# Gate and up weights four rows to a partition, with three of a pair's four units in one 4 MB transfer each from the sixth pair of experts on

## The chip, the cores and the metric

The kernel runs on one core of one Trainium2 chip. The metric is the device time of one execution in microseconds (us); a median over runs is given. The profile is of one execution. Engines are named as the profile names them: PE is TensorE (PEld its weight loads), DVE is VectorE, ACT is ScalarE, POOL is GpSimd, SP is the sync engine, which issues nearly all transfers. A pair, below, is a pair of experts.

## What is computed

One layer of an encoder block for 256 tokens of 1024 channels, all in float32: an attention and pooling part (the first 190 us), and then a mixture of experts, where the rest of the time goes. Each of the 32 experts has a gate/up matrix (1024 by 2048, 8 MB) and a down matrix (1024 by 1024, 4 MB). Each token goes to 4 experts.

```python
gu = xb @ w_gate_up[e] + b_gate_up[e]
gate = jnp.minimum(gu[:, :EXPERT_DIM], SWIGLU_LIMIT)
up = jnp.clip(gu[:, EXPERT_DIM:], -SWIGLU_LIMIT, SWIGLU_LIMIT)
act = gate * jax.nn.sigmoid(SWIGLU_ALPHA * gate) * (up + 1.0)
return act @ w_down[e] + b_down[e]
```

The outputs are scaled by the token's gate and summed into the residual `x`.

## The kernel before

**Weights and slots.** All weights of the experts are read once, in units of 2 MB, into ten slots of 16 KB in each of 128 partitions. A gate/up matrix is four units (`gu_slot`, eight slots for the two experts of a pair), a down matrix two (`dn_slot`, two slots). Gate/up unit `i` holds rows 256i to 256i+255 of the matrix; partition p of the slot has rows 2p and 2p+1 of these, which lie together in memory, so each partition's piece is one run of 16 KB (`gu_src`, L231). A down unit has four rows of 4 KB to a partition, also one run of 16 KB. Row r of the weights multiplies channel r of the activations, so which rows lie in a partition sets which channels the kernel has to gather into it: `gather_first`, `gather_rest` and `gather` (L1265 to L1319) turn `xn` with a matmul whose stationary operand is every second channel, and `g2_t`, the channel gains of the second norm, is loaded by POOL in the same order (L390).

**The order of the work on PE.** `pair` (L1431) runs one turn: `gate_up(1)` for the second expert of this pair (units 4 to 7), with the scatter of earlier results after k 1 and k 3, a turn of the gates after k 4 and the gather for the next pair after k 6; `down(0, 0)`, `turn`, `down(0, 1)` for the first expert; `gate_up(0)` for the first expert of the next pair (units 0 to 3) with two more scatters; and `down(1, 0)`, `turn`, `down(1, 1)`. Each unit is two values of k. `gate_up` waits for `gu_in[s]` before the first of the two (L1369) and raises `gu_used[s]` after the second. Turn 1 stands alone, a loop runs turns 2 to n-1 (`pe.Fori(2, n)`, L1468) and the last turn n has its own form, in which `x_in_sums` takes the gather's place and `add_to_sums` and `last_down` end the kernel. n is 16 here.

**The order of the transfers.** SP issues them in the order in which PE wants them, each when its slot is free. The first eight gate/up units and two down units are loaded while the attention part ends and frees their slots: units 0 to 7 in this order (L306 to L319), then the down units (L320). The next gate/up load waits for `first_used`, which PE raises after the first k of `gate_up` (L344). Up to pair `EARLY` = 5 the order is spelled out; then a loop (L362) issues for each pair

```python
gates_a(here, q)
downs_b(sp.snap(2 * (it % PAIRS)), q2)
gates_b(here, q)
downs_a(here, q3)
```

where `gates_a` and `gates_b` are four units each, `downs_a` and `downs_b` two. After the loop the last expert's down matrix goes into `gu_slot[0]` and `gu_slot[1]`, in three transfers (L370, L373).

Of the kernel before, what the change touches and what calls it, by code (L numbers as in the profile page):

```python
# [5 lines left out]
P = 128  # L6
SEQ = 256
D = 1024
NB = SEQ // P
KC = D // P  # L10
# [52 lines left out]
def block_kernel(nc, x_d, pos_d, w_in, w_a, w_b, w_out, mix_d, router_d, w_gu, w_dn, b_dn,  # L63
# [6 lines left out]
    with ctx:  # L70
        def sb(name, width, dt=f32, parts=P):
            return ctx.enter_context(nc.sbuf_tensor(name, [parts, width], dt))

        def sem(name):
            return ctx.enter_context(nc.semaphore(name))
# [7 lines left out]

        slot = [sb(f"slot{s}", UW) for s in range(SLOTS)]
        gu_slot = [slot[s] for s in (0, 1, 6, 7, 3, 9, 4, 8)]
        dn_slot = [slot[5], slot[2]]
# [88 lines left out]
        p1_copied, gate_done = sem("p1_copied"), sem("gate_done")  # L175
        gu_in = [sem(f"gu_in{s}") for s in range(GU_SLOTS)]
        gu_used = [sem(f"gu_used{s}") for s in range(GU_SLOTS)]
        dn_in = [sem(f"dn_in{j}") for j in range(DN_SLOTS)]
# [43 lines left out]
        def pre_unit_src(u):  # L222
# [6 lines left out]
            return w[r:r + 2 * P, :].rearrange("(k p) n -> p k n", p=P), 2 * D  # L229

        def gu_src(e, i):  # L231

            return w_gu[bass.ds(e * D + i * 2 * P, 2 * P), :].rearrange("(p k) n -> p (k n)", k=2)

# [25 lines left out]
        def _(sp):  # L260
# [52 lines left out]
            load_gu(4, 1)  # L313
            sp.wait_ge(job_ready, 2 * (BJ_WB + NB))
            load_gu(5, 1)
            units_used(18)
            load_gu(6, 1)
            sp.wait_ge(job_ready, 2 * (BJ_WA + NB))
            load_gu(7, 1)  # L319
            for j in range(DN_SLOTS):  # L320
# [8 lines left out]
            def gates_b(expert, used, first=0, end=4):  # L329
                for i in range(first, end):  # L330
                    sp.wait_ge(gu_used[4 + i], used)
                    load_gu(4 + i, expert + 1)

            def downs_a(expert, used):
# [27 lines left out]
            with sp.Fori(EARLY - 1, n - 1) as it:  # L362
                here, q, q2, q3 = sp.snap(2 * ((it + 1) % PAIRS)), sp.snap(it + 1), sp.snap(2 * it + 2), sp.snap(2 * it + 3)
                gates_a(here, q)
                downs_b(sp.snap(2 * (it % PAIRS)), q2)
                gates_b(here, q)
                downs_a(here, q3)
# [12 lines left out]
        @block.gpsimd  # L380
        def _(pool_e):
            pool_e.wait_ge(unit_in[0], 16)
            pool_e.dma_start(consts[:, P:K_W], consts_d[:, P:K_W]).then_inc(small_in, 16)
            pool_e.dma_start(rows[:, :], rows_d.to_broadcast([P, R_W])).then_inc(small_in, 16)
            pool_e.dma_start(posi[:, :], pos_d).then_inc(small_in, 16)
            pool_e.wait_ge(unit_in[2], 16)
            pool_e.dma_start(bands_t, bands_d).then_inc(late_in, 16)
            pool_e.dma_start(mixw, mix_d.rearrange("g c d -> c g d")).then_inc(late_in, 16)
            pool_e.dma_start(bgu_t[:, :], bgu_d).then_inc(bgu_in, 16)
            for k in range(2):  # L390
                for m in range(2):
                    pool_e.dma_start(g2_t[64 * m:64 * m + 64, k:KC:2],
                                     cols_d[k:P:2, P_G2 + m:P_G2 + KC:2], allow_slow_non_contiguous=True).then_inc(g2_in, 16)

            pool_e.wait_ge(t_ready, TJ_M + 4)
            for h in range(2):
                pool_e.dma_start(bd_sb[E * h:E * h + E, :], b_dn[:, 512 * h:512 * h + 512]).then_inc(bd_in, 16)

            pool_e.wait_ge(merged_ready, NB)
            pool_e.dma_start(rw, router_d.rearrange("(k p) e -> p k e", p=P)).then_inc(rw_in, 16)  # L400
# [149 lines left out]
        def _(dve):  # L550
# [412 lines left out]

            dve.wait_ge(g2_in, 64)
            take_xgT(1)
# [20 lines left out]
        def _(pe):  # L986
            MM = nc.tensor.matmul
            for j in range(DN_SLOTS):
                pe.sem_inc(dn_used[j], 1)
            for j in range(4):  # L990
                pe.sem_inc(done[f"Y{j}"], 2)
# [273 lines left out]
            def gather_first(h):  # L1265
                pe.wait_ge(sel_ready, 1)
                pe.wait_ge(xn_ready, 2 * NB)
                for k in range(4):
                    c0 = (4 * h + k) // 2 * 2 * P + k % 2
                    MM(XY[h][:, k * P:k * P + P], xn[:, 0, c0:c0 + 2 * P - 1:2], selb[:, 0:P], start=k == 0, stop=False)  # L1270

            def gather_rest():
                pe.wait_ge(sel_ready, 2)
                pe.wait_ge(xn_ready, 3 * NB)
                for h in range(2):
                    for k in range(4):
                        c0 = (4 * h + k) // 2 * 2 * P + k % 2
                        ins = MM(XY[h][:, k * P:k * P + P], xn[:, 1, c0:c0 + 2 * P - 1:2], selb[:, P:2 * P], start=False, stop=k == 3)
                    ins.then_inc(done[f"X{h}"], 1)
# [28 lines left out]
            def gather(count, freed):  # L1308

                pe.wait_ge(sel_ready, count)  # L1310
                for h in range(2):
                    pe.wait_ge(read[f"Y{2 + h}"], freed)
                for h in range(2):
                    for k in range(4):
                        c0 = (4 * h + k) // 2 * 2 * P + k % 2
                        for b in range(NB):
                            ins = MM(XY[h][:, k * P:k * P + P], xn[:, b, c0:c0 + 2 * P - 1:2], selb[:, b * P:b * P + P],  # L1317
                                     start=b == 0, stop=b == NB - 1)
                    ins.then_inc(done[f"X{h}"], 1)  # L1319
# [40 lines left out]

            def gate_up(e, landed, copied, taken, between, whole_first=False):
                for h in range(2):
                    pe.wait_ge(gu_copied[h], copied)
                for k in range(KC):
                    s = 4 * e + k // 2
                    if e == 0 and k % 4 == 0:
                        pe.wait_ge(read[f"X{k // 4}"], taken)
                    if k % 2 == 0:
                        pe.wait_ge(gu_in[s], landed)  # L1369
# [60 lines left out]

            def pair(count, turn_no, first, last):  # L1431
                q, q1 = count(turn_no + 0), count(turn_no + 1)
# [8 lines left out]
                else:  # L1441
                    between.append((6, lambda: gather(count(turn_no + 2), q3)))
                gate_up(1, in1, q2, None, between)
                down(0, 0, dn_a, q2, q2)
                turn(q3, q2)
                down(0, 1, dn_a, q2, q2)
                if not last:
                    gate_up(0, in2, q3, q1, [(1, lambda: scatter_a(0, q1, q3, q4, first)), (3, lambda: scatter_a(1, q1, q3, q4, first))])
                if last:
# [17 lines left out]
            n = pe.value_load(n_t[0:1, 0:1], min_val=PAIRS, max_val=4 * PAIRS)  # L1467
            with pe.Fori(2, n) as it:  # L1468
                pair(pe.snap, it, False, False)
            pair(pe.snap, n, False, True)  # L1470
            pe.wait_ge(last_copied, 1)
# [51 lines left out]
```

## Time and profile before

| what | value |
| --- | --- |
| median of 3 runs | 1099.01 us (1098.03 to 1099.58) |
| time of the profiled execution | 1100.01 us |
| span of the profiled execution | 1098.2 us |
| PE busy | 1051.5 us (96%) |
| weights and inputs read from memory | 429.03 MB |
| gate/up transfers of 2 MB, median issue to landing | 127, 29.4 us |

The span is the time from the first to the last instruction of the profiled execution; the 1.8 us between it and the execution's time lie around the instructions. A busy share is an average over stages with different limits. In the queries below, a stretch of time is given in us from the span's start.

### The profile page before, as it was taken

To read this page: it belongs to the slowest core of one execution; us is meant where nothing else is said; L and a number is where in the kernel's file an instruction comes from. 1 tells how busy PE (TensorE), PEld (TensorE's weight loads), DVE (VectorE), ACT (ScalarE), POOL (GpSimd) and SP (SyncE) were. 2 spreads that over 40 slices of the span, in tenths; PEclk is the share of its full clock that TensorE was granted. 3 is DMA by queue.
4 is the path that set the end of the run, shared out by engine and by line. 5 is a ranking of instruction groups with operands and counts; after the bars stand their busy time and mean duration, and the time that the engine had idled before them with its cause. 6 is when DMAs were issued, how large, how long until landed. Compare 5 with 4: busy or idle time off the path is not lost.

```text
span 1098.2 us, 12167 instructions
## 1 busy us (share of the span) xinstructions
PE 1051.5 (96%) x4822; PEld 425.5 (39%) x4822; DVE 356.0 (32%) x675; ACT 117.6 (11%) x211; POOL 8.2 (1%) x17
## 2 busy tenths in 40 slices
PE   9999999999999999999999999898989899999997
PEld 6445446333433434343433333242424242333322
DVE  4797224122222232322322322222222222122222
ACT  3115112100000000000000000000000000000001
POOL 2000000000000000000000000000000000000000
PEclk9999999999999999999999999999999999999999
DMA  9905784999999999999999999999999999999996
GB/s 326 376 28 192 290 363 176 407 422 416 427 429 429 429 428 429 428 429 427 428 429 429 428 428 429 428 428 428 429 429 428 428 430 428 428 428 428 429 428 251
DMA packets 40561, 430.33 MB, mean 392 GB/s; under 512 B 4048, under 2 KB 6224, under 8 KB 15712
## 3 DMA queue, kind: packets, MB, share of 16 engines
q1 hardware_dynamic: 39568, 428.11, 93.0%
q0 software_dynamic: 688, 1.91, 0.5%
q8 instruction: 12, 0.20, 0.1%
q10 hardware_dynamic: 288, 0.08, 0.0%
q14 instruction: 5, 0.04, 0.0%
HBM read 429.03 MB, written 1.05 MB: 392 GB/s over the span
## 4 chain that ended last, share of the span: by engine, by line
PE 63%; DMA 34%; SPq 2%; issue 1%; DVE 0%; ACT 0%; DVEq 0%
DMA slot<-w_gate_up_dram 33%; PE bank L1373 21%; PE bank L1400 14%; PE bank L1317 5%; PE bank L1185 4%; PE bank L1038 4%; PE bank L1062 4%; PE bank L1389 2%; PE bank L1334 2%; PE bank L1295 1%; SPq L290 1%; PE bank L1005 1%; PE bank L1427 1%; DMA x<-x_dram 1%; PE bank L1358 0%
## 5 line engine op out<-in xcount | busy, mean ns | idle before, releaser
L1373 PE MATMUL bank<-slot,scr 128*64 128x512 f32 x2048 | 469.9, 598 | 24.9 <-DMA slot<-w_gate_up_dram 24.7
L1373 PEld LDWEIGHTS bank<-slot,scr 128*64 128x64 f32 x2048 | 136.5, 136 | 322.8 <-issue 258.1
L1400 PE MATMUL bank<-slot,scr 128*64 128x512 f32 x992 | 225.4, 596 | 11.3 <-DMA slot<-w_down_dram 10.5
L947 DVE TENSOR_TENSOR x<-bank,x 128x512 f32<-128x512 f32 x120 | 77.3, 686 | 233.5 <-PE bank L1334 233.5
L1400 PEld LDWEIGHTS bank<-slot,scr 128*64 128x64 f32 x992 | 67.7, 137 | 142.3 <-issue 118.5
L922 DVE COPY scr<-bank 128x512 f32<-128x512 f32 x32 | 22.1, 692 | 288.2 <-PE bank L1373 288.2
L928 DVE TENSOR_TENSOR scr<-bank,bgu 128x512 f32<-128x512 f32 x64 | 41.2, 686 | 106.0 <-PE bank L1389 106.0
L1334 PE MATMUL bank<-scr 64*128 64x512 f32 x240 | 67.7, 641 | 0.0
L1317 PEld LDWEIGHTS bank<-scr,xn 128*128 128x128 f32 x480 | 57.7, 196 | 12.2 <-issue 12.2
L514 ACT ACTIVATE scr<-bank 128x512 f32<-128x512 f32 x32 | 19.1, 598 | 399.0 <-PE bank L1373 399.0
L1317 PE MATMUL bank<-scr,xn 128*128 128x128 f32 x480 | 60.5, 285 | 0.0
L1038 PE MATMUL bank<-slot,scr 128*128 128x290 f32 (+1 forms) x128 | 43.8, 501 | 0.4 <-DVE scr L573 0.3
L1389 PEld LDWEIGHTS bank<-consts,scr 128*128 128x128 f32 x256 | 33.4, 210 | 26.9 <-issue 26.9
L1389 PE MATMUL bank<-consts,scr 128*128 128x128 f32 x256 | 39.4, 297 | 0.9 <-ACT scr L514 0.9
L518 ACT ACTIVATE scr<-scr 128x512 f32<-128x512 f32 x32 | 20.2, 631 | 183.4 <-DVE scr L932 183.4
L1334 PEld LDWEIGHTS bank<-scr 64*128 64x128 f32 x240 | 18.1, 184 | 48.6 <-issue 48.6
L1038 PEld LDWEIGHTS bank<-slot,scr 128*128 128x128 f32 x128 | 24.0, 190 | 19.2 <-issue 15.3
L526 ACT ACTIVATE scr<-bank 128x512 f32<-128x512 f32 x16 | 9.6, 597 | 189.7 <-PE bank L1358 189.7
L1062 PE MATMUL bank<-slot 128*128 128x512 f32 x64 | 28.7, 596 | 0.0
L1185 PE MATMUL bank<-slot 128*128 128x512 f32 x56 | 26.4, 600 | 0.0
L522 ACT ACTIVATE scr<-bank 128x512 f32<-128x512 f32 x31 | 18.5, 598 | 45.3 <-PE bank L1400 45.3
L936 DVE SCALAR_TENSOR_TENSOR scr<-scr 128x512 f32<-128x512 f32 x32 | 22.2, 693 | 3.3
(202 smaller groups left out, 489.9 us busy)
## 6 DMA issues: line engine op xcount, KB each, us to landing
slot<-w_gate_up_dram SPq DMA_DIRECT2D x127, 2048.0 KB, 29.4
slot<-w_down_dram SPq DMA_DIRECT2D x63, 2048.0 KB, 22.8
slot<-w_in_dram SPq DMA_DIRECT2D x12, 1024.0 KB, 15.5
slot<-w_out_dram SPq DMA_DIRECT2D x4, 1024.0 KB, 7.3
slot<-w_in_dram SPq DMA_DIRECT2D x4, 580.0 KB, 7.8
slot<-w_branch_pool_dram SPq DMA_DIRECT2D x2, 1024.0 KB, 7.3
slot<-w_branch_attn_dram SPq DMA_DIRECT2D x2, 1024.0 KB, 6.2
slot<-w_gate_up_dram SPq DMA_DIRECT2D x2, 1024.0 KB, 5.8
```

Of the source, the lines that this page charges most:

```text
L922: V.tensor_copy(gu_sb[:, 512:1024], GB[1][:, :]).then_inc(gu_copied[1], 1)
L928: V.tensor_tensor(gu1[:, 4 * h:4 * h + 4, :, :], v4(TU[h][:, :], 4, 2), bias.unsqueeze(3).to_broadcast([P, 4, 2, T]), ALU.add).then_inc(re ...
L936: V.scalar_tensor_tensor(out=up1, in0=up1, scalar=1.0, in1=gu1[:, :, 0, :], op0=ALU.add, op1=ALU.mult).then_inc(prod_ready, 1)
L947: V.tensor_tensor(x[:, b, 512 * h:512 * h + 512], XY[h][:, :], x[:, b, 512 * h:512 * h + 512], ALU.add).then_inc(read[f"Y{j}"], 1)
L1038: ins = MM(bank[PAIR[j][b]][:, 0:n], hT[:, kc, b * P:b * P + P], w[:, k, :], start=kc == 0, stop=kc == KC - 1)
L1062: ins = MM(bank[PAIR[j][h]][:, :], lhs[:, k, b * P:b * P + P], w[:, k % 2, 512 * h:512 * h + 512], start=k == 0, stop=k == nk - 1)
L1185: ins = MM(acc[:, :], lhs[:, k, :], rhs[:, k, :], start=k == 0, stop=k == 3)
L1317: ins = MM(XY[h][:, k * P:k * P + P], xn[:, b, c0:c0 + 2 * P - 1:2], selb[:, b * P:b * P + P], start=b == 0, stop=b == NB - 1)
L1334: MM(XY[h][:, :], selgT[T * h:T * h + T, SEQ * e + b * P:SEQ * e + b * P + P], dsb[T * h:T * h + T, 512 * e:512 * e + 512], start=not with ...
L1373: ins = MM(GB[h][T * g:T * g + T, :], xgT[:, k, T * e:T * e + T], gu_slot[s][:, c0:c0 + 512], start=k == 0, stop=k == KC - 1)
L1389: ins = nc.tensor.transpose(TU[h][:, k * P:k * P + P], gu_sb[:, c0:c0 + 4 * P - 3:4], ident)
L1400: ins = MM(DB[T * h:T * h + T, :], actT[e][:, c, :], v3(dn_slot[j][:, :], 4)[:, k, 512 * h:512 * h + 512], start=c == 0, stop=c == KC - 1)
```

## The change

The memory of the ten slots becomes one tensor, so that two neighbouring slots can be written by one transfer. Four rows of a gate/up matrix, 32 KB, now lie over one partition of two neighbouring slots (a tile); a unit is half of such a tile, 16 KB out of every 32 KB. The slots of gate/up units 5, 6 and 7 change places, and with them the order of the first loads. From the loads for the sixth pair on, SP issues tiles 0, 1 and 2 (units 0 and 1, 2 and 3, 4 and 5) as one transfer of 4 MB each, with a semaphore of its own, and units 6 and 7 as before. PE waits for the whole tile before its first k. PE's one loop over turns becomes a loop over turns 2 to 4, turn 5 by itself, a loop over turns 6 to 15, and the last turn. The gathers take every fourth channel, and the gains are loaded by 16 small transfers in place of 4.

```diff
-        slot = [sb(f"slot{s}", UW) for s in range(SLOTS)]
-        gu_slot = [slot[s] for s in (0, 1, 6, 7, 3, 9, 4, 8)]
+        ring = sb("ring", SLOTS * UW)
+        slot = [ring[:, UW * s:UW * s + UW] for s in range(SLOTS)]
+        gu_slot = [slot[s] for s in (0, 1, 6, 7, 3, 4, 8, 9)]
+        gu_tile = [ring[:, UW * s:UW * s + 2 * UW] for s in (0, 6, 3, 8)]
...
+        big_in = [sem(f"big_in{t}") for t in range(3)]
...
+        def tile_src(e, t):
+
+            return w_gu[bass.ds(e * D + t * 4 * P, 4 * P), :].rearrange("(p k) n -> p (k n)", k=4)
+
         def gu_src(e, i):

-            return w_gu[bass.ds(e * D + i * 2 * P, 2 * P), :].rearrange("(p k) n -> p (k n)", k=2)
+            whole = tile_src(e, i // 2)
+            return whole[:, UW * (i % 2):UW * (i % 2) + UW]
...
             load_gu(4, 1)
             sp.wait_ge(job_ready, 2 * (BJ_WB + NB))
+            load_gu(7, 1)
+            units_used(18)
             load_gu(5, 1)
-            units_used(18)
+            sp.wait_ge(job_ready, 2 * (BJ_WA + NB))
             load_gu(6, 1)
-            sp.wait_ge(job_ready, 2 * (BJ_WA + NB))
-            load_gu(7, 1)
...
+            def tiles(expert, t, used):
+                for i in range(2):
+                    sp.wait_ge(gu_used[2 * t + i], used)
+                sp.dma_start(gu_tile[t], tile_src(expert + t // 2, t % 2)).then_inc(big_in[t], 16)
...
-                gates_a(here, q)
+                tiles(here, 0, q)
+                tiles(here, 1, q)
                 downs_b(sp.snap(2 * (it % PAIRS)), q2)
-                gates_b(here, q)
+                tiles(here, 2, q)
+                gates_b(here, q, 2, 4)
                 downs_a(here, q3)
...
-            for k in range(2):
-                for m in range(2):
-                    pool_e.dma_start(g2_t[64 * m:64 * m + 64, k:KC:2],
-                                     cols_d[k:P:2, P_G2 + m:P_G2 + KC:2], allow_slow_non_contiguous=True).then_inc(g2_in, 16)
+            for k in range(4):
+                for m in range(4):
+                    pool_e.dma_start(g2_t[32 * m:32 * m + 32, k:KC:4],
+                                     cols_d[k:P:4, P_G2 + m:P_G2 + KC:4], allow_slow_non_contiguous=True).then_inc(g2_in, 16)
...
+            for t in range(3):
+                pe.sem_inc(big_in[t], 16 * EARLY)
...
-                        c0 = (4 * h + k) // 2 * 2 * P + k % 2
+                        c0 = 4 * P * h + k
                         for b in range(NB):
-                            ins = MM(XY[h][:, k * P:k * P + P], xn[:, b, c0:c0 + 2 * P - 1:2], selb[:, b * P:b * P + P],
+                            ins = MM(XY[h][:, k * P:k * P + P], xn[:, b, c0:c0 + 4 * P - 3:4], selb[:, b * P:b * P + P],
                                      start=b == 0, stop=b == NB - 1)
...
-                    if k % 2 == 0:
+                    if whole and k % 4 == 0 and s < 6:
+                        pe.wait_ge(big_in[2 * e + k // 4], landed)
+                    elif k % 2 == 0 and not (whole and s < 6):
                         pe.wait_ge(gu_in[s], landed)
...
-            with pe.Fori(2, n) as it:
+            with pe.Fori(2, EARLY) as it:
                 pair(pe.snap, it, False, False)
-            pair(pe.snap, n, False, True)
+            pair(int, EARLY, False, False, whole_a=True)
+            with pe.Fori(EARLY + 1, n) as it:
+                pair(pe.snap, it, False, False, whole_b=True, whole_a=True)
+            pair(pe.snap, n, False, True, whole_b=True)
```

## Rows read from the trace of the kernel before

**Rows 1.** The page: PE's totals, and the memory rate in 40 slices.

```profile
PE 1051.5 (96%) x4822; PEld 425.5 (39%) x4822; DVE 356.0 (32%) x675; ACT 117.6 (11%) x211; POOL 8.2 (1%) x17
...
GB/s 326 376 28 192 290 363 176 407 422 416 427 429 429 429 428 429 428 429 427 428 429 429 428 428 429 428 428 428 429 429 428 428 430 428 428 428 428 429 428 251
```

**Rows 2.** Stretches of 58.7 us: busy time (and instructions) by engine, clock, DMA, GB/s.

```profile
434.80:493.50 58.70, 58.70 (x300) 24.54 (x300) 15.87 (x28) 4.25 (x7) 0.00 (x0) 1.00 1.01 428
...
669.60:728.30 58.70, 54.59 (x262) 20.26 (x260) 15.86 (x28) 4.21 (x8) 0.00 (x0) 1.00 1.01 428
```

**Rows 3.** Chain of waits, 419 to 473 us: start, duration, what.

```profile
419.08 3.43 PE bank L1373 x16
...
428.21 1.87 PE bank L1373 x8
...
430.67 3.58 PE bank L1373 x16
...
448.27 3.43 PE bank L1373 x16
...
457.40 7.02 PE bank L1373 x32
...
472.60 3.43 PE bank L1373 x16
```

**Rows 4.** Timeline of PE, 1002 to 1090 us: start, duration, [idle before, who ended it].

```profile
1002.79 1.94 PE L1373 MATMUL bank<-slot,scr 128*64 128x512 f32 x8 [0.19 <-DMA slot<-w_gate_up_dram]
...
1007.68 1.94 PE L1373 MATMUL bank<-slot,scr 128*64 128x512 f32 x8 [0.50 <-DMA slot<-w_gate_up_dram]
...
1056.62 3.65 PE L1373 MATMUL bank<-slot,scr 128*64 128x512 f32 x16 [0.18 <-DMA slot<-w_gate_up_dram]
...
1061.51 1.94 PE L1373 MATMUL bank<-slot,scr 128*64 128x512 f32 x8 [0.18 <-DMA slot<-w_gate_up_dram]
...
1066.67 1.94 PE L1373 MATMUL bank<-slot,scr 128*64 128x512 f32 x8 [0.76 <-DMA slot<-w_gate_up_dram]
...
1082.42 7.09 PE L1427 MATMUL bank<-slot,scr 128*64 128x512 f32 x32
```

**Rows 5.** What SP waited for, 350 to 1045 us: us in total, times, longest.

```profile
SPq L293 <- PE bank L1400: 599.0, 48, 24.0
```

**Rows 6.** Timeline of SP, 1000 to 1098 us.

```profile
1024.37 1.91 SPq L290 DMA_DIRECT2D slot<-w_gate_up_dram  x4
1045.78 5.22 SPq L293 DMA_DIRECT2D slot<-w_down_dram  x2
```

**Rows 7.** DMA view, stretches 600 to 1050 us and 26 to 51 us.

```profile
DMA packets 13243, 192.86 MB, mean 429 GB/s; under 512 B 1472, under 2 KB 1472, under 8 KB 1472
...
DMA packets 4792, 9.70 MB, mean 388 GB/s; under 512 B 148, under 2 KB 148, under 8 KB 4791
```

**Rows 8.** The page, DMA queues: the instruction queue's packets, MB, share.

```profile
q8 instruction: 12, 0.20, 0.1%
```

**Rows 9.** DMA view, 1055 to 1066 us, the instruction queue.

```profile
q8 instruction: 1, 0.02, 0.6%
```

**Rows 10.** Source view, L1317 and L1389: duration of one in ns (min/median/max), first and last start.

```profile
L1317 PEld LDWEIGHTS bank<-scr,xn x480: 193/196/197, 218.0 to 1013.2; 128*128 128x128 f32 x160
...
L1389 PEld LDWEIGHTS bank<-consts,scr x256: 195/212/219, 203.9 to 1076.6; 128*128 128x128 f32 x128
```

**Rows 11.** Timeline, 184 to 191 us, and a stretch of 2 us in it.

```profile
184.81 2.15 PE L1278 MATMUL bank<-scr,xn 128*128 128x128 f32 x16 [0.45 <-DVE scr L862]
...
189.07 0.33 SPq L345 DMA_DIRECT2D slot<-w_gate_up_dram  x1
...
188.00:190.00 2.00, 2.00 (x12) 0.84 (x10) 1.73 (x7) 0.00 (x0) 0.00 (x0) 1.00 0.00 0
```

**Rows 12.** POOL: its timeline at 14 us, and its longest wait.

```profile
13.77 2.46 POOL L392 DMA_DIRECT2D g<-cols_dram  x4
...
POOL scr L397 <- PE bank L1005: 138.9, 1, 138.9
```

More of the change, by code:

```diff
@@ L962, in pair @@
                     make_sel(after2)
-            dve.wait_ge(g2_in, 64)
+            dve.wait_ge(g2_in, 256)
             take_xgT(1)
@@ L1268, in gather_first @@
                 for k in range(4):
-                    c0 = (4 * h + k) // 2 * 2 * P + k % 2
-                    MM(XY[h][:, k * P:k * P + P], xn[:, 0, c0:c0 + 2 * P - 1:2], selb[:, 0:P], start=k == 0, stop=False)
+                    c0 = 4 * P * h + k
+                    MM(XY[h][:, k * P:k * P + P], xn[:, 0, c0:c0 + 4 * P - 3:4], selb[:, 0:P], start=k == 0, stop=False)
             def gather_rest():
@@ L1276, in gather_rest @@
                     for k in range(4):
-                        c0 = (4 * h + k) // 2 * 2 * P + k % 2
-                        ins = MM(XY[h][:, k * P:k * P + P], xn[:, 1, c0:c0 + 2 * P - 1:2], selb[:, P:2 * P], start=False, stop=k == 3)
+                        c0 = 4 * P * h + k
+                        ins = MM(XY[h][:, k * P:k * P + P], xn[:, 1, c0:c0 + 4 * P - 3:4], selb[:, P:2 * P], start=False, stop=k == 3)
                     ins.then_inc(done[f"X{h}"], 1)
@@ L1314, in gather @@
                     for k in range(4):
-                        c0 = (4 * h + k) // 2 * 2 * P + k % 2
+                        c0 = 4 * P * h + k
                         for b in range(NB):
-                            ins = MM(XY[h][:, k * P:k * P + P], xn[:, b, c0:c0 + 2 * P - 1:2], selb[:, b * P:b * P + P],
+                            ins = MM(XY[h][:, k * P:k * P + P], xn[:, b, c0:c0 + 4 * P - 3:4], selb[:, b * P:b * P + P],
                                      start=b == 0, stop=b == NB - 1)
@@ L1359, in gates_by_slot, with gate_up @@
                 ins.then_inc(done["S"], 1)
-            def gate_up(e, landed, copied, taken, between, whole_first=False):
+            def gate_up(e, landed, copied, taken, between, whole_first=False, whole=False):
                 for h in range(2):
@@ L1429, in last_down, with pair @@
                 ins.then_inc(dn_used[1], 1)
-            def pair(count, turn_no, first, last):
+            def pair(count, turn_no, first, last, whole_b=False, whole_a=False):
                 q, q1 = count(turn_no + 0), count(turn_no + 1)
@@ L1442, in pair @@
                     between.append((6, lambda: gather(count(turn_no + 2), q3)))
-                gate_up(1, in1, q2, None, between)
+                gate_up(1, in1, q2, None, between, whole=whole_b)
                 down(0, 0, dn_a, q2, q2)
@@ L1447, in pair @@
                 if not last:
-                    gate_up(0, in2, q3, q1, [(1, lambda: scatter_a(0, q1, q3, q4, first)), (3, lambda: scatter_a(1, q1, q3, q4, first))])
+                    gate_up(0, in2, q3, q1, [(1, lambda: scatter_a(0, q1, q3, q4, first)), (3, lambda: scatter_a(1, q1, q3, q4, first))], whole=whole_a)
                 if last:
```

## The prediction

> **What bounds the kernel now.** I read the page first. PE is busy 96% of the span and the memory rate is flat at 428 to 429 GB/s from the twelfth slice on [rows 1], so two resources look full, and the share can't say which one sets the end. Stretches of 58.7 us tell them apart [rows 2]: up to about 550 us PE has no idle time and more instructions fit a stretch than one turn of the loop needs (300 against 262), so PE runs ahead at its own pace; later PE is busy 54.6 of 58.7 us, and the stream still runs at the same 428 GB/s. The chain of waits gives PE's own pace: one turn from 419.08 to 472.60 us, 53.5 us [rows 3]. The timeline gives the other: unit 7 of two successive turns starts at 1007.68 and 1066.67 us, 59.0 us apart [rows 4]. So from some 550 us to the last weights the stream of transfers is the bound, and PE waits a little for each unit. What sets the end is: when the stream starts, how long it runs, and how much PE work is left when the last pieces have landed.
>
> Two facts about the stream. First, its step. Between 600 and 1050 us, 13243 - 1472 = 11771 packets of 16 KB went through 16 engines in 450 us: 450 x 16 / 11771 = 611.7 ns each, eight to an engine and unit, so 4.89 us per unit [rows 7]. Nothing is left over for a cost per transfer. Second, its depth: SP hardly waits for anything but down slots (599 us in 48 waits) [rows 5], since the gate/up slots of a turn have always been used by the time the down slots ahead of them in SP's order are free. A gate/up unit lands 29.4 us, six steps, after its issue (the table above). The change therefore issues nothing later: a tile's two waits are met when SP reaches them.
>
> **Longer rows in the stream.** No row shows a 32 KB packet. The cost of one is bounded by the packets that are there: between 26 and 51 us, 4644 packets with a mean of 2088 bytes took 25 x 16 / 4644 = 86.1 ns each, beside 611.7 ns for 16384 bytes [rows 7]. A straight line through both has 9.3 ns per packet and the rest by bytes. A tile in 32 KB packets needs 8 per engine where two units need 16, so it saves 8 x 9.3 = 75 ns. The loop issues 3 tiles in each of 11 turns: 33 x 0.075 = 2.5 us. The bounds: nothing, if the hardware cuts a row at 16 KB, and 3.3 us, if the line's constant is a third too low. I take 2.3 us. The ordinary units now read 16 KB out of each 32 KB; the nearest strided reads are those of 26 to 51 us, rows of `w_in` at a pitch of 14.6 KB (3652 floats), and even if all of the line's constant of 9.3 ns were due to their stride it would be 1.5% of a 16 KB packet; since the contiguous units fit the same line, I take nothing for it here.
> [...]
>
> **The hold of a whole tile.** PE now waits for 4 MB before the first of four k. The second half of a tile lands when the second unit landed, so the start of its four k is put off by one step, 4.89 us less what PE waited anyway. In the bound stretch that costs nothing as long as PE catches up in each turn. Count from the landing of tile 2 (units 4, 5). From there to the end of `down(0, 1)` PE needs 448.27 - 419.08 = 29.2 us [rows 3], and the next tile 0 lands six steps later, 29.4 us. Tile 0's work is 9.1 us (two units and their scatters), against 9.8 to tile 1. From tile 1 it needs 15.2 us (472.60 - 457.40), and tile 2 lands four steps later, 19.6. So PE is back at a standstill each turn, with 4.4 us to spare. The down slots come free later than before (in the last turn before from 1045.78 us on [rows 6]), but at least 10 us ahead of the time when the stream gets to them, because two tiles are still queued in front. The stream doesn't run dry.
>
> At the end nothing comes after to catch up in. Before, PE starts unit 5 at 1056.62 us and unit 7 at 1066.67, each as it lands, and from there on works without waiting for a transfer [rows 4]. Now it starts unit 4 when unit 5 is there, at 1056.62, and needs 9.13 us for units 4 and 5 with two scatters (428.21 - 419.08), 2.46 for k 4 with the turn of the gates, and 1.79 for k 5, half of the 3.58 [rows 3]. That makes 1070.00 us for the start of unit 7, against 1066.67: **3.3 us later**, and all that follows (`last_down` at 1082.42 and the sums) is PE's own work, so it moves by the same. Bounds: 2.5 (if a restart after a wait runs tighter than the back-to-back rows) to 4.9, a full step.
>
> **The start of the stream.** Between the first loads and the reload there is a hole, zero GB/s from 188 to 190 us: SP waits for `first_used` and issues at 189.07 us [rows 11]. That follows from `gather_rest` (16 matmuls, 2.15 us from 184.81), which is on the path. Its stationary reads go from every second to every fourth channel. L1317 loads every second element and takes 196 ns, `turn` at L1389 loads every fourth and takes 212 [rows 10]. So 16 loads x 16 ns is 0.26 us at most, 0 if the matmuls hide it; I take 0.2. In the loop 32 loads x 16 ns = 0.5 us a turn more, which the 4.4 us to spare take up; without that cover it would be 5 us over ten turns.
> The trace agrees in direction with the Trainium skill (SBUF — State Buffer, Specifications): a 16-byte line wants at least two hits for full bandwidth, and a step of four floats hits each line once. If that meant half speed, 196 ns a load would become 392 and the start would move 3.1 us; the row of `turn` has 212.
>
> **Code.** PE's program has 9644 records of matmuls and loads [rows 1], 522 to a turn [rows 2], so about 1290 before the turns and, with three written turn bodies, 2860 in all; 12 instruction fetches brought them in [rows 8]. The two new bodies (turn 5 and the second loop) are 1044 more, so four or five fetches, most inside the saturated stream. One such fetch, between 1055 and 1066 us, took 0.6% of 11 us x 16 engines, 1.06 us of engine time [rows 9], and there the step from unit 6 to unit 7 (1061.51 to 1066.67) is 5.16 us, 0.27 longer than 4.89 [rows 4]. A transfer has landed when its slowest engine is done, so a fetch costs nothing (on an engine with time in hand) up to 1.06 us. Five cost 0 to 5 us; by the one seen, 1.3. I take 1.0.
>
> **At nothing.** The order of the first loads (4, 7, 5, 6): same bytes, slots and waits; all of them are issued before `gather_rest` (184.81 us, [rows 11]), and `gate_up(1)` comes a whole `gate_up` after it. If unit 6 were late, PE would wait a step, 4.9 us, once, at a time when the stream, not PE, sets the end. The 12 further gain loads: 2.46 / 4 = 0.6 us each on POOL [rows 12], 7.4 us, ahead of a wait of 138.9 us; uncovered, 7.4 us. 22 fewer issues on SP, which idles 599 us.
>
> **The sum.** -2.3 + 3.3 + 0.2 + 1.0 = +2.2 us. On the profiled execution's span of 1098.2 that is 1100.4, on its 1100.01 us 1102.2; it stood 1.0 above the median of 1099.01, which becomes **1101.2 us**. About 0.2% (2.2 us) is what a measurement of this kernel can tell from no change, so the forecast sits on that edge.
>
> **The rivals.**
> *Rows are cut at 16 KB* (the change doesn't do what it says): nothing is saved, +4.5 us, 1103.5. For it: every packet of the stream is 16 KB or less. Against it: 16 KB is also the longest row that was asked for.
> *Transfers have a fixed cost in the stream* (faster): 33 fewer ones save it. The nearest row is SP's step between issues, 1.91 / 4 = 0.48 us [rows 6], so 33 x 0.48 = 15.8 us: 1101.2 - 15.8 = 1085.4. It gives a faster kernel from 4.4 / 33 = 0.13 us per transfer on. Against it: eight packets make the whole step [rows 7]. The Trainium skill (DMA: Bandwidth & Descriptors, Anatomy of one DMA) has such a cost, about 2 us per transfer, mostly completion; with six transfers queued the trace shows it overlapped.
> *The pitch slows the half-tile units*: 128 - 66 in tiles - 8 first loads = 54 of them lie in the saturated stream. At the 388 GB/s of 26 to 51 us [rows 7] each takes 5.4 us, 0.5 more: +27, 1128. Nothing in the trace shows such a pitch.
> *The hold isn't caught up*: if a turn ends later than the stream allows, each of ten turns loses up to a step of 4.9: +49, 1150. It decides only if PE needs 4.4 us more per turn than rows 3 say.
>
> **How the numbers follow.** The forecast has 0.68 (own range 1099.5 to 1103.0, about evenly on both sides of the edge), cut rows 0.14, a fixed cost 0.08, pitch 0.05, the hold 0.05. The range 1098.8 to 1104.6 takes in the first two with the bounds of fetches and restart. Slower: 0.30 + 0.14 + 0.05 + 0.05 = 0.54; same: 0.36; faster: 0.08 + 0.02.
>
> **What the profile after would show.** Packets over 16 KB and fewer of them, and a rate near 432 GB/s in stretches with tiles; PE idle only before tiles, about 4 us before tile 2; unit 7 of the last turn with no wait before it; `last_down` 13.4 + 15.8 = 29.1 us after tile 2's first k; 16 or 17 fetches; L1317's successor near 212 ns. It would be wrong if the rate didn't rise, if the stretch of full PE work before 550 us grew, or if PE waited for unit 6 or 7 in the last turn.

## The result, and the profile after

The changed kernel takes 1119.41 us (median of 4 runs, 1119.22 to 1119.83) against 1099.02 us before: a ratio of 1.0184, 95% interval 1.0172 to 1.0197, 20.4 us slower. The forecast was 1101.2 us, within 1098.8 to 1104.6. The way was right, the size was not, by far. The reason is one term, the stationary loads of the gathers, which the forecast had at 0.2 us for the start and at nothing for the turns.

The page of the changed kernel: its span, PE's totals, the memory rate in 40 slices, the queues (packets, MB, share), and three groups of instructions (busy, mean ns of one | idle before).

```profile
span 1117.8 us, 12107 instructions
...
PE 1101.7 (99%) x4822; PEld 486.6 (44%) x4822; DVE 355.6 (32%) x675; ACT 117.7 (11%) x211; POOL 14.2 (1%) x29
...
GB/s 332 362 34 197 295 328 171 410 384 399 389 421 385 421 387 426 375 430 430 430 430 429 437 424 438 423 435 426 432 429 432 430 432 430 430 430 429 426 430 225
...
q1 hardware_dynamic: 34816, 428.11, 91.5%
...
q8 instruction: 16, 0.26, 0.1%
...
L1392 PE MATMUL bank<-ring,scr 128*64 128x512 f32 x2048 | 466.2, 597 | 6.4 <-DMA ring<-w_gate_up_dram 6.4
...
L1334 PEld LDWEIGHTS bank<-scr,xn 128*128 128x128 f32 x480 | 113.1, 329 | 12.2 <-issue 12.2
...
L1408 PEld LDWEIGHTS bank<-consts,scr 128*128 128x128 f32 x256 | 33.3, 210 | 26.9 <-issue 26.9
```

Against [rows 1], PE has the same 4822 matmuls and 50.2 us more of them, PEld 61.1 us more. L1334 is the gather, L1317 of before. Its stationary load takes 329 ns; it took 196 [rows 10], and the forecast had 212. The matmuls with gate/up weights (L1392) take as long as ever, and PE waits only 6.4 us before them; `turn` (L1408) has the 210 ns it had. And the memory rate, flat from the twelfth slice before, dips to 375 to 389 GB/s in every other slice from the ninth to the seventeenth.

The chain of waits has one gather of the loop whole (start, duration), between units 6 and 7:

```profile
449.14 3.58 PE bank L1392 x16
452.73 7.66 PE bank L1334 x32
460.39 1.87 PE bank L1392 x8
```

7.66 us a turn where it was 3.97 (32 matmuls of L1317 at 434.25 us in the chain of before); PE's own turn (two starts of the same step, 609.20 and 666.42 us) is 57.2 us in place of 53.5 [rows 3].

Stretches of 20 us, columns as in [rows 2], first of the changed kernel and then of the kernel before:

```profile
230.00:250.00 20.00, 20.00 (x92) 6.79 (x90) 6.61 (x11) 1.83 (x3) 0.00 (x0) 1.00 0.90 371
250.00:270.00 20.00, 20.00 (x96) 6.89 (x92) 6.68 (x13) 1.83 (x3) 0.00 (x0) 1.00 0.99 396
...
350.00:370.00 20.00, 20.00 (x94) 6.83 (x92) 6.01 (x10) 1.23 (x2) 0.00 (x0) 1.00 0.91 366
...
450.00:470.00 20.00, 20.00 (x94) 12.11 (x92) 5.04 (x9) 1.23 (x2) 0.00 (x0) 1.00 0.87 357
```

```profile
230.00:250.00 20.00, 20.00 (x90) 6.19 (x88) 4.14 (x7) 1.11 (x2) 0.00 (x0) 1.00 1.00 426
250.00:270.00 20.00, 20.00 (x94) 6.82 (x90) 7.97 (x15) 1.83 (x3) 0.00 (x0) 1.00 1.01 415
...
350.00:370.00 20.00, 20.00 (x96) 6.94 (x94) 6.68 (x13) 1.82 (x3) 0.00 (x0) 1.00 1.01 429
...
450.00:470.00 20.00, 20.00 (x94) 6.83 (x92) 4.52 (x7) 0.60 (x1) 0.00 (x0) 1.00 1.01 429
```

The last two columns (the share of time in which the transfer engines were busy, and GB/s) are the point: PE has no idle time in either kernel, but now the transfer engines have. SP can refill a slot only when PE has used it. That a whole turn of 57.2 us is still shorter than the stream's 58.7 doesn't help, for two reasons that SP's timeline shows. Down weights have two slots, and SP issues in order, so what counts is the time from one pair of down loads to the next. And up to pair `EARLY` the spelled-out order puts four gate/up units between two pairs of down loads, then three: six and five units with the down units, 29.4 and 24.5 us of stream at 4.89 us each, 53.8 us a turn. SP's timeline before the change:

```profile
253.80 5.08 SPq L293 DMA_DIRECT2D slot<-w_down_dram  x2
258.92 13.41 SPq L290 DMA_DIRECT2D slot<-w_gate_up_dram  x4
282.99 5.08 SPq L293 DMA_DIRECT2D slot<-w_down_dram  x2
288.11 8.03 SPq L290 DMA_DIRECT2D slot<-w_gate_up_dram  x3
307.32 5.07 SPq L293 DMA_DIRECT2D slot<-w_down_dram  x2
```

and after it, with a stretch of 2 us at the end of the long half:

```profile
261.20 5.07 SPq L301 DMA_DIRECT2D ring<-w_down_dram  x2
266.31 13.41 SPq L298 DMA_DIRECT2D ring<-w_gate_up_dram  x4
294.08 5.08 SPq L301 DMA_DIRECT2D ring<-w_down_dram  x2
299.20 8.03 SPq L298 DMA_DIRECT2D ring<-w_gate_up_dram  x3
318.42 5.07 SPq L301 DMA_DIRECT2D ring<-w_down_dram  x2
...
294.00:296.00 2.00, 2.00 (x14) 1.35 (x14) 1.02 (x2) 0.00 (x0) 0.00 (x0) 1.00 0.63 131
```

Before, PE hands the down slots back after 29.2 and 24.3 us, which just feeds the stream. The gather lies in the longer half. Now that half takes 32.9 us, and the stream, with 29.4 us of work in hand, runs dry for some 3.5 us before each of the down loads at 294.08, 351.30, 408.51 and 465.96 us. By the same sum the first hole, before 234.76 us, is 2.9 us. That estimate makes 17 us in all. From the loop on there are six units to each half, 58.7 us of stream for PE's 57.2: PE's shorter half, 24.3 us, now leaves 5 us of transfers queued for the longer one, and the holes end. Over the 13 such stretches from 230 to 490 us the rates add up to 5201 GB/s in place of 5552, which at 428 is (5552 - 5201) x 20 / 428 = 16.4 us of stream lost. Later the stream is the bound again and goes at its own rate, so nothing of that comes back. The first wait of PE for a weight transfer in the pairs is at 781.91 us in the changed kernel (572.10 before), and from there on there is one in each of the six turns left. The timeline of PE in the last two turns shows it:

```profile
1015.92 3.65 PE L1392 MATMUL bank<-ring,scr 128*64 128x512 f32 x16 [1.06 <-DMA ring<-w_gate_up_dram]
...
1074.43 3.65 PE L1392 MATMUL bank<-ring,scr 128*64 128x512 f32 x16 [1.07 <-DMA ring<-w_gate_up_dram]
...
1103.63 7.09 PE L1446 MATMUL bank<-ring,scr 128*64 128x512 f32 x32
```

PE waits for tile 2 each time and its turns are 58.5 us apart, the stream's pace. So the sum, in the profile's own times: the reload starts 3.7 us later (SP's issue at 192.78 us against 189.07 [rows 11]), the holes cost 16.4, the longer rows give about 2.3 back, and the last turn's hold adds up to 3.3: 21.1 us for the start of `last_down`, which moved by 1103.63 - 1082.42 = 21.2 [rows 4]. The first three terms can be read by themselves: unit 5 is there 1074.43 - 1056.62 = 17.8 us later. The two spans are only 19.6 us apart, because in the profiled execution before the change the output took longer: 6.1 us from the first output transfer's issue (1092.08 us) to the end, where the changed kernel (1113.30 us) and all the other profiles have 4.4 to 4.5.

### The profile page after: what moved, and what is told of

Read it like the earlier page. It is cut to its first block, busy times and chain, and to the rows that moved or that the text cites. A ratio compares the mean times of both kernels' runs of the same rounds, so it can differ in the third digit from the quotient of the medians.

```text
span 1117.8 us, 12107 instructions
## 1 busy us (share of the span) xinstructions
PE 1101.7 (99%) x4822; PEld 486.6 (44%) x4822; DVE 355.6 (32%) x675; ACT 117.7 (11%) x211; POOL 14.2 (1%) x29
## 4 chain that ended last, share of the span: by engine, by line
PE 85%; DMA 14%; SPq 0%; issue 0%; ACT 0%; DVE 0%; DVEq 0%
PE bank L1392 33%; PE bank L1419 16%; DMA ring<-w_gate_up_dram 13%; PE bank L1334 10%; PE bank L1351 5%; PE bank L1202 4%; PE bank L1055 4%; PE bank L1079 4%; PE bank L1408 3%; PE bank L1312 1%; PE bank L1022 1%; PE bank L1375 1%; PE bank L1446 1%; DMA ring<-w_in_dram 1%; PE bank L1295 0%; PE bank L1434 0%
## 5 line engine op out<-in xcount | busy, mean ns | idle before, releaser
L1392 PE MATMUL bank<-ring,scr 128*64 128x512 f32 x2048 | 466.2, 597 | 6.4 <-DMA ring<-w_gate_up_dram 6.4
L1392 PEld LDWEIGHTS bank<-ring,scr 128*64 128x64 f32 x2048 | 137.9, 137 | 297.5 <-issue 283.2
L1419 PE MATMUL bank<-ring,scr 128*64 128x512 f32 x992 | 224.9, 595 | 0.0
L1419 PEld LDWEIGHTS bank<-ring,scr 128*64 128x64 f32 x992 | 68.4, 137 | 127.7 <-issue 124.0
L1334 PEld LDWEIGHTS bank<-scr,xn 128*128 128x128 f32 x480 | 113.1, 329 | 12.2 <-issue 12.2
L1334 PE MATMUL bank<-scr,xn 128*128 128x128 f32 x480 | 116.0, 400 | 0.0
L1408 PEld LDWEIGHTS bank<-consts,scr 128*128 128x128 f32 x256 | 33.3, 210 | 26.9 <-issue 26.9
L1055 PE MATMUL bank<-ring,scr 128*128 128x290 f32 (+1 forms) x128 | 43.8, 501 | 0.8 <-DMA ring<-w_in_dram 0.8
L1408 PE MATMUL bank<-consts,scr 128*128 128x128 f32 x256 | 39.3, 297 | 0.9 <-ACT scr L529 0.9
L1055 PEld LDWEIGHTS bank<-ring,scr 128*128 128x128 f32 x128 | 24.0, 190 | 19.6 <-issue 15.3
L1079 PE MATMUL bank<-ring 128*128 128x512 f32 x64 | 28.7, 596 | 0.0
L1202 PE MATMUL bank<-ring 128*128 128x512 f32 x56 | 26.4, 600 | 0.0
```

The costliest lines, as they stand in the source:

```text
L1055: ins = MM(bank[PAIR[j][b]][:, 0:n], hT[:, kc, b * P:b * P + P], w[:, k, :], start=kc == 0, stop=kc == KC - 1)
L1079: ins = MM(bank[PAIR[j][h]][:, :], lhs[:, k, b * P:b * P + P], w[:, k % 2, 512 * h:512 * h + 512], start=k == 0, stop=k == nk - 1)
L1202: ins = MM(acc[:, :], lhs[:, k, :], rhs[:, k, :], start=k == 0, stop=k == 3)
L1334: ins = MM(XY[h][:, k * P:k * P + P], xn[:, b, c0:c0 + 4 * P - 3:4], selb[:, b * P:b * P + P], start=b == 0, stop=b == NB - 1)
L1392: ins = MM(GB[h][T * g:T * g + T, :], xgT[:, k, T * e:T * e + T], gu_slot[s][:, c0:c0 + 512], start=k == 0, stop=k == KC - 1)
L1408: ins = nc.tensor.transpose(TU[h][:, k * P:k * P + P], gu_sb[:, c0:c0 + 4 * P - 3:4], ident)
```

## The experiments

Theory G says that all beyond the forecast is the gathers' stationary loads. Rival H puts it to the tiles, their hold or the pitch. The first four runs tell them apart.

**e1: the changed kernel, gathers at every second channel**

```diff
-                        c0 = 4 * P * h + k
-... xn[:, b, c0:c0 + 4 * P - 3:4] ...
+                        c0 = (4 * h + k) // 2 * 2 * P + k % 2
+... xn[:, b, c0:c0 + 2 * P - 1:2] ...
```

> The changed kernel whose gathers read every second channel, as before the change; the channels are then the wrong ones for the four-row weights, and nothing else differs. Theory G (the gathers' stationary loads): the gather falls back from 7.7 to 4.0 us a turn and the stream starts 3 us earlier, so the time is what was forecast without the gather's term: 1099 + 2 = 1101 us, 1099.5 to 1103. Rival H (the hold of whole tiles, or the 32 KB pitch of the half-tile units): these are untouched, so 1112 to 1119 us, and the stream still has its holes between 230 and 480 us.

1102.96 us, ratio 1.0039 (1.0024 to 1.0054). G's value, at the top of its range: 16.5 of the 20.4 us are gone with this one line, which stands in three places, and its memory rate has no such dips (426, 409, 428, 429 from the ninth slice on).

**e2: the kernel before, gathers at every fourth channel**

The same edit the other way round, in the kernel before.

> The kernel before, whose gathers read every fourth channel (the wrong ones for its two-row weights); nothing else differs. Theory G: PE's turn grows from 53.5 to 57.2 us, the stream starts 3 us later and gets holes while PE is the bound: 1114 to 1120 us. Rival H: 1099 to 1104 us, since a turn of 57.2 us is still under the stream's 58.7.

1118.42 us, ratio 1.0174 (1.0159 to 1.0190). The stride alone, with neither tiles nor four-row weights nor new turn bodies, makes 19 of the 20 us, holes in the stream included: its slices of the memory rate go 378, 404, 387, 421, 386, 419 like those above. "A turn of 57.2 us is still under the stream's 58.7" and so harmless, as H had it, is refuted: the sum over a turn is right, but the half of it with the gather is longer than the stream's six units.

**e3: the changed kernel with the activations written in the gather's order**

```diff
-  nc.scalar.activation(xn[:, b, :], x[:, b, :], ACT.Copy, scale=...)
+  nc.scalar.activation(xn[:, b, :].rearrange("q (h k p) -> q h k p", h=2, k=4),
+                       x[:, b, :].rearrange("q (h p k) -> q h k p", h=2, k=4), ACT.Copy, scale=...)
...
-  xn[:, b, 4 * P * h + k:4 * P * h + k + 4 * P - 3:4]
+  xn[:, b, (4 * h + k) * P:(4 * h + k) * P + P]
```

> The changed kernel in full, but ACT writes the normed activations in the order of the gather (channel 512h + 4p + k at place 512h + 128k + p), so each gather's stationary operand is 128 neighbouring floats. Theory G: a load takes 190 ns as in the other matmuls, the gather 3.9 us a turn, and the time is 1099.5 to 1103 us, or 0.3 us under the run that reads every second channel; ACT's two copies from the strided source may cost up to 1 us at the start. Rival H: 1112 to 1119 us.

1102.20 us, ratio 1.0032 (1.0020 to 1.0044). It is the change with the cost of its gather taken away. G's value again. The ratio puts it 3.5 us above the kernel before (2.2 to 4.8 by its interval), where the forecast's other terms had made 2.0 (2.2 less the gather's 0.2).

**e4: the load against its step**

In the kernel before, the eight groups of the loop's gather read 128 channels at steps of 1 to 8 floats (`xn[:, b, 0:127 * s + 1:s]`), each on its own line. Only the loads are read from it; its one execution took 1110.68 us.

> The kernel before, whose gather in the loop takes 128 channels at a step of 1, 2, 3, 4, 5, 6, 7 and 8 floats in its eight groups (the wrong channels), each on a line of its own, to measure a stationary load against its step. If what counts is how many 16-byte lines the 128 floats touch, a load takes 190 ns at 1, 196 at 2, 330 at 4, some 250 at 3, and 330 from 4 to 8. If it is the span in bytes, it grows on from 4 to 8: 600 ns and more at 8.

The source view of each line, PEld (ns: min/median/max); L1315 is step 1, L1330 step 8:

```profile
L1315 PEld LDWEIGHTS bank<-scr,xn x60: 186/190/192, 218.4 to 1021.5; 128*128 128x128 f32 x60
...
L1317 PEld LDWEIGHTS bank<-scr,xn x60: 195/197/200, 218.9 to 1022.0; 128*128 128x128 f32 x60
...
L1319 PEld LDWEIGHTS bank<-scr,xn x60: 251/261/263, 219.3 to 1022.6; 128*128 128x128 f32 x60
...
L1321 PEld LDWEIGHTS bank<-scr,xn x60: 317/330/330, 220.0 to 1023.5; 128*128 128x128 f32 x60
...
L1324 PEld LDWEIGHTS bank<-scr,xn x60: 314/315/319, 220.9 to 1024.4; 128*128 128x128 f32 x60
...
L1326 PEld LDWEIGHTS bank<-scr,xn x60: 316/317/319, 221.8 to 1025.2; 128*128 128x128 f32 x60
...
L1328 PEld LDWEIGHTS bank<-scr,xn x60: 325/327/328, 222.7 to 1026.2; 128*128 128x128 f32 x60
...
L1330 PEld LDWEIGHTS bank<-scr,xn x60: 334/334/335, 223.6 to 1027.1; 128*128 128x128 f32 x60
```

190, 197, 261, 330, and then 315 to 334: it isn't the span that counts. The time rises as long as fewer floats share 16 bytes and stops where each has its own, as expected of the number of 16-byte lines touched; the small steps between 315 and 334 that count doesn't explain. That is the direction of the rule of the Trainium skill (SBUF — State Buffer, Specifications) that the forecast cited: with two hits to a line (step 2) the load is nearly at full speed, with one (step 4) it takes 330/190 = 1.74 times as long.

What is left of e3's excess was then taken apart. Theory T: the hold in the last turn, and a clock that falls in it. Rival R: the new turn bodies, or the pitch.

**e5: e3 with 2 MB units and no holds**

`tiles(here, t, q)` is replaced by `gates_a(here, q)` and `gates_b(here, q)`, and PE waits for `gu_in[s]` in all turns.

> The changed kernel with ordered activations (the run e3 before), but every unit in a transfer of its own, 2 MB, waited for by itself; four-row weights, slots and PE's two loops stay. Theory T: what e3 still loses is the last turn's hold (3.3 us, and 1.7 us for 16 matmuls at half the clock after PE's idle 3.3 us), less 2.4 us that the 32 KB packets give. So 1102.2 - 5.0 + 2.4 = 1099.6 us, 1099 to 1100.3. Rival R (the new turn bodies and their fetches, or the 32 KB pitch, cost the 3 us): 1102 us or more.

1099.01 us, ratio 0.9997 (0.9988 to 1.0006): T. The four-row layout, the 32 KB pitch, the new bodies and the order of the first loads cost nothing that can be told, which leaves room for about 1 us.

**e5h: e5, with the holds put back**

```diff
+                    if whole and k % 4 == 0 and s < 6:
+                        pe.wait_ge(gu_in[s], landed)
+                        pe.wait_ge(gu_in[s + 1], landed)
+                    elif k % 2 == 0 and not (whole and s < 6):
+                        pe.wait_ge(gu_in[s], landed)
```

> The same with 2 MB units, but PE waits before the first k of units 0, 2 and 4 for that unit and its neighbour, from turn 5 or 6 on, as it would for a whole tile: the hold by itself, without the longer rows. Theory T: 5.0 us over the run with separate waits, 1104.6 us; the first matmuls of the last turn run at half the clock after an idle of 3 to 4 us. Rival: if the hold costs only its delay, 3.3 us, 1102.9; if PE catches up, no difference.

1104.42 us, ratio 1.0043 (1.0029 to 1.0056), 5.4 us over e5 by the medians. The hold costs more than the delay of 3.3 us. Timeline of PE in this run's last turn:

```profile
1057.59 5.35 PE L1391 MATMUL bank<-ring,scr 128*64 128x512 f32 x16 [4.32 <-DMA ring<-w_gate_up_dram]
...
1063.93 3.65 PE L1391 MATMUL bank<-ring,scr 128*64 128x512 f32 x16
```

After 4.32 us of idle time the first 16 matmuls take 5.35 us, the next 16, the same work, 3.65. The granted clock is the cause; in e3, the same place (stretches of 5 us; the column before the last two is the clock):

```profile
1050.00:1055.00 5.00, 2.42 (x12) 0.57 (x8) 3.38 (x8) 1.23 (x2) 0.00 (x0) 1.00 0.90 380
1055.00:1060.00 5.00, 4.31 (x12) 1.30 (x14) 0.00 (x0) 0.00 (x0) 0.00 (x0) 0.66 1.00 426
1060.00:1065.00 5.00, 5.00 (x24) 1.51 (x22) 1.29 (x2) 0.00 (x0) 0.00 (x0) 1.00 0.99 423
```

0.66 over five microseconds is a stay at the lower of the two levels, 1.2 GHz, and then the return to 2.4. In the kernel before, PE's longest wait for a unit in these turns is 1.25 us, and the page's clock row is full throughout.

**e9: e3 with tiles 0 and 1 only**

Units 4 to 7 are one by one again (`gates_b(here, q)`, and the hold only where `s < 4`).

> The run e3 with tiles 0 and 1 in 4 MB transfers as before and units 4 to 7 one by one, so that no hold lies in the last turn; 22 tiles in place of 33. Theory T: 1102.2 - 5.0 + 0.8 (11 tiles less at 0.073 us) = 1098.0 us, faster than before the change by about 1 us, and no long idle time ahead of unit 4. Rival R: 1101.5 to 1103.

1097.90 us, ratio 0.9989 (0.9980 to 0.9998). It is the fastest of all, 1.2 us below the kernel before; the interval just excludes no difference. But a hold still sets its end: PE idles 3.54 us ahead of tile 0 at 1026.27 us, takes 6.57 us for the next 16 matmuls, and from there on never waits for a transfer again, with unit 4 of the last turn at 1053.57 us. The expectation had no hold left in the last turn; its number came out all the same, and not by the path that it named.

**e7: the kernel before with ordered activations**

> The kernel before with the normed activations written in the order of its own gather (two rows to a partition): nothing of the change. A load takes 190 ns in place of 196, so the gather is 0.1 us shorter a turn and the start of the stream comes 0.1 us earlier at most; ACT's strided copies may take that back. 1098.8 to 1099.5 us, no difference that can be told.

1098.71 us, ratio 0.9995 (0.9986 to 1.0004). No difference that can be told, as expected (the median is 0.1 us under the range): e9's gain isn't the order of the activations by itself.

**e8: the kernel before, every fourth channel in the loop only**

> The kernel before, with only the loop's gathers reading every fourth channel (the wrong ones); the two gathers ahead of the mixture of experts read every second one. It splits the 19.2 us of the run in which all do. If the extra time is PE's work alone (15 gathers of 3.7 us on top of a PE that was idle for about 36 us, and 3.5 us of later start), this has all but the start: 1118.4 - 3.5 = 1114.9 us, 1114 to 1116. If the holes in the stream set the time by themselves and the start counts for nothing, 1118.

1115.96 us, ratio 1.0154 (1.0138 to 1.0169). The loop's gathers alone make 17 us, and they make it by the holes: the stream starts at 189.04 us as before the change, and the dips are there (386, 378, 381, 378, 382 GB/s in every other slice from the ninth on). The two gathers ahead of the loop add some 2 us, the rest of e2's 19, though the intervals of the two ratios overlap. Its value is just inside the range of the first view, 1 us above its centre.

**e5c: e5 with PE's one loop of before**

> The changed kernel with ordered activations, 2 MB transfers throughout and PE's one loop of before: what is left of the change is the four-row layout, the slots, the order of the first loads and the 16 small loads of the gains. It differs from the run with 2 MB units only in PE's two further turn bodies and their four instruction fetches. By the forecast's term (1.0 us for the fetches) 1098.0 us; if the fetches cost nothing, 1099.0, and the layout costs nothing either; if the 32 KB pitch cost anything, above 1099.5.

1098.83 us, ratio 0.9997 (0.9988 to 1.0006), the same as e5. Four fetches and two bodies cost nothing that can be told, and neither does the layout. The two intervals are about 1 us wide to each side, so the forecast's 1.0 us for the fetches isn't excluded.

**e11: e3 with tile 1 only**

> The run with tiles 0 and 1, but only tile 1 (units 2 and 3) in one transfer of 4 MB, 11 tiles in place of 22. The longer rows give 0.8 us less, 1097.9 + 0.8; but in that run tile 0's hold and the half clock after it made PE start the last turn's unit 4 at 1053.6 us, 2.9 after it landed, and unit 6 and 7 without a wait, so up to 1.7 us of it should go. 1097.0 to 1098.7 us. If it comes out above 1099, holding tile 1 costs the same as tile 0.

1099.61 us, ratio 1.0000 (0.9991 to 1.0009): a miss, above the expected 1097.0 to 1098.7. The kernel before took 1099.41 us beside this run and 1099.05 beside e9, so 0.4 of the 1.7 us between the medians of e9 and e11 lie in the kernel before as well. The trace shows what the expectation had wrong. PE at the last tile 1:

```profile
1037.87 8.54 PE L1391 MATMUL bank<-ring,scr 128*64 128x512 f32 x32 [3.55 <-DMA ring<-w_gate_up_dram]
```

32 matmuls of 7.09 us take 8.54, and PE then never waits for a transfer again, as in e9. But it comes to unit 4 of the last turn at 1054.42 us, 0.85 later than in e9 and not earlier, and the two profiled executions are 0.9 us apart. The hold of tile 1 ends 11.6 us later than that of tile 0, and leaves PE that much less time to catch up before the last turn. This is read from one execution of each, and the intervals of e9 and e11 overlap.

## Why the prediction was wrong, step by step

- **The step that failed: "16 loads x 16 ns" and "32 loads x 16 ns = 0.5 us", in the paragraph on the start of the stream.** The difference of 16 ns was taken between L1317, loads of ordinary matmuls, and L1389, loads of transposes. These are two kinds of load, and each has its own base. Both bases stood in the same trace, here in the source views of L1038 and L1358 of the kernel before, which read neighbouring floats:

```profile
L1038 PEld LDWEIGHTS bank<-slot,scr x128: 186/190/192, 7.2 to 51.0; 128*128 128x128 f32 x128
```

```profile
L1358 PEld LDWEIGHTS bank<-consts,scr x32: 138/140/142, 213.8 to 1063.5; 128*128 128x128 f32 x32
```

  So a step of two cost a matmul's load 196 - 190 = 6 ns, and a step of four cost a transpose's load 212 - 140 = 72 ns, half as much again. Compared like with like, the nearest row of the trace gave 72 ns and a factor of 1.5 for what had been called 16. The changed kernel shows more, 134 ns and 1.7. The forecast then used its 16 ns to set the rule of the Trainium skill (SBUF — State Buffer, Specifications) aside. Its own figure for that rule, 196 ns more a load, was too high, but nearer than 16: it had the start 3.1 us later, and 3.7 was measured. In the loop it would have been 32 x 196 = 6.3 us a turn, more than the 4.4 to spare, which the forecast didn't work out.
- **The second failure: the cover of 4.4 us a turn.** It was counted in the stretch where the stream is the bound, and there it held (PE waits 1.07 us a turn in the changed kernel, from 781.91 us on). Before that PE is the bound, and the stream lives on the slots that PE hands back. "The stream doesn't run dry" was checked for the later turns alone, by waits of SP from 350 us on [rows 5]; 16.4 us were lost between 230 and 490 us. The forecast had the two numbers that say so: PE needs 29.2 us from tile 2 to the end of `down(0, 1)`, the half of the turn with the gather, and the stream takes 29.4 for its six steps. That is 0.2 us to spare and not 4.4; the added work was 3.7. The sign that the forecast named for being wrong, a longer stretch of full PE work, is there: from 572.10 to 781.91 us. "5 us over ten turns", named for the case without cover, was too small by far.
- **The start**: 0.2 us was forecast; the reload is issued 3.7 us later. The 32 loads of the two gathers there take 330 ns in place of 196, 4.3 us in all of which waits hid some, and part of `gather_rest` ran at the lower clock: a granted 0.89, 0.50 and 0.75 in the stretches of 2 us from 186 to 192 us. How much of the 3.7 is the clock's stays open.
- **Longer rows: right.** 32 KB packets came. From 600 to 1050 us, 193.53 MB went through in place of 192.86 [rows 7], 0.35% more, which over the some 620 us from the first tile to the last is 2.2 us; 2.3 was forecast. The mean rate is 430 GB/s, where a rate near 432 had been named. "Rows are cut at 16 KB" is refuted. The DMA view of the changed kernel:

```profile
DMA packets 9954, 193.53 MB, mean 430 GB/s; under 512 B 1104, under 2 KB 1104, under 8 KB 1104
```

- **The hold at the end: right, and more.** From tile 2's first k to `last_down` 29.1 us were forecast; it took 1103.63 - 1074.43 = 29.2 in the changed kernel. The 3.3 us was the delay alone; with a fast gather PE idles 3.28 us first in e3 (4.32 in e5h), and the clock adds 1.7 (5.35 - 3.65). The forecast's "back at a standstill each turn" missed that a standstill has a price. In the changed kernel itself that price wasn't paid: the slow gather left only 1.07 us of idle time.
- **Fetches**: 16 in place of 12, as forecast (16 or 17); 1.0 us was forecast; e5 against e5c shows none that can be told, to about 1 us.
- **At nothing**: nothing that can be told for the order of the loads, the pitch and the gains (e5, e5c).
- **A fixed cost per transfer**: the rival's 0.48 us is refuted, since 33 joined transfers gave 2.2 us in all and not 15.8. Whether these 0.07 us a tile belong to the packets, as forecast, or to the transfer was not told apart: each tile is one transfer less and eight packets less on each engine. The 2 us that the forecast cites there from the Trainium skill (DMA: Bandwidth & Descriptors, Anatomy of one DMA) are stated for transfers issued by GpSimd; here SP issues them.

With the failing term out, the sum would have been 2.0 us. With the fetches at nothing and the clock's 1.7 us put in it is 2.7, and e3 shows 3.5 (2.2 to 4.8 by its interval).

## What to carry to other kernels

A layout chosen for the transfers also sets the step at which an engine reads the other operand: price that read first, against rows of the same kind of instruction. Where ten slots are shared between a stream and its reader, find out in which part of the run each is the bound, and compare the two between one refill of the scarcest slot and the next, not over a whole turn; slack of the later part doesn't cover work added in the earlier. If two transfers are joined, look at the last joined piece before the end: the wait for it is time that nothing wins back, and the reader's longer idle time can cost it its clock. With the last one left out (e9, which has the ordered activations too) the change was 1.2 us faster than before, just clear of noise.

## What the runs showed of the hardware

- A float32 stationary load of 128x128 takes 190, 197, 261 and 330 ns at steps of 1, 2, 3 and 4 floats, and 315 to 334 ns at 5 to 8 (e4).
- PE's granted clock fell to its lower level, 1.2 GHz, in most places where a tile was waited for: after idle times of 2.54 to 4.32 us in e3, e5h and e9, 16 matmuls of 3.65 us took 5.1 to 6.6. After 1.25 us in the kernel before and 2.06 to 2.29 us in e3, e5h and e9 they took 3.65. Once, in e3 at 529.12 us, they took 3.65 after an idle time of 3.81 us, with a granted clock of 1.00; so the length of the idle time alone doesn't decide it.
- The clock also fell during the gathers at step four ahead of the experts, with no idle time over 0.46 us (0.50 from 188 to 190 us in the changed kernel, from 190 to 192 in e2; in e3 it stayed at 1.00).
- A row of 32 KB is carried whole, in fewer packets (9954 in place of 13243 from 600 to 1050 us): with half of its bytes in 4 MB tiles the stream is 0.35% faster.
